# A two-layer decoder trunk on one core: picks in groups of two, a mixer row in every second group, the rotation table beside attention rows, and routings moved between light rows

## The reference, cut to what matters

```
for l in range(2):                                   # DEPTH; x is 256 tokens x 1024
    h = rms_norm(x, norm1_g[l]); proj = h @ w_in[l]  # q, k, v, forget logits, pool, ssm
    att  = forgetting_attention(q, k, v, f_logit + f_bias)      # 8 heads x 64
    pool = multiscale_pool(u_pool)                   # trailing windows 2, 4, 8, 16
    ssm  = s5_mixer(u_ssm)                           # diagonal complex scan, gelu, GLU
    x = x + concat(norm(att), norm(pool), norm(ssm)) @ w_out[l]
    h = rms_norm(x, norm2_g[l])                      # PEER: 128*128 experts, 8 heads, top 16
    q = h @ peer_wq[l]; scores = q . peer_keys[l]    # two halves of 128 keys per head
    e, g = product-key top 16 of each head, softmax  # 8 x 16 = 128 picks per token
    x = x + sum over picks of g * gelu(h . peer_u[l][e]) * peer_v[l][e]
```

## Time and profile before

| engine | busy us | share of the span | instructions |
|---|---|---|---|
| PE (matmul) | 1049.1 | 68% | 6790 |
| PEld (weight load) | 532.8 | 34% | 6790 |
| DVE (VectorE) | 1083.2 | 70% | 2485 |
| ACT (ScalarE) | 575.1 | 37% | 1768 |
| POOL (GpSimd) | 619.7 | 40% | 571 |

### The profile page before, as it was taken

How to read it: one execution, slowest core, us unless ns; L and a number is a source line. 1 busy time by engine, 2 the same in 40 slices (tenths; PEclk the granted TensorE clock), 3 DMA queues, 4 the chain that set the end, 5 groups by cost and what they waited for, 6 DMA issues and landing times. The chain is left out here.

```text
span 1546.1 us, 19439 instructions
## 1 busy us (share of the span) xinstructions
PE 1049.1 (68%) x6790; PEld 532.8 (34%) x6790; DVE 1083.2 (70%) x2485; ACT 575.1 (37%) x1768; POOL 619.7 (40%) x571
## 2 busy tenths in 40 slices
PE   8898656785854668776775667788588465565555
PEld 6685312333531334332552334333255111111111
DVE  8777998646999685654789767564579965444444
ACT  5544433623444433441544431354234432221222
POOL 0034345442753533443343433444243354455441
PEclk9999877887986988787897788889698777667767
DMA  9289999999999999999999999999999999999997
GB/s 381 89 326 421 420 421 420 421 421 405 422 421 368 411 422 421 421 421 421 409 421 421 421 421 421 421 422 420 422 386 421 421 421 422 421 421 422 421 421 304
DMA packets 86642, 623.55 MB, mean 403 GB/s; under 512 B 10000, under 2 KB 10128, under 8 KB 11792
## 3 DMA queue, kind: packets, MB, share of 16 engines
q0 software_dynamic: 73728, 536.90, 83.7%
q1 hardware_dynamic: 12816, 85.41, 13.4%
HBM read 621.23 MB, written 1.05 MB: 402 GB/s over the span
## 5 line engine op out<-in xcount | busy, mean ns | idle before, releaser
L583 POOL DMA_INDIRECT slots<-experts,idx x512 | 593.2, 1159 | 886.5 <-PE psum L1830 709.9
L1427 DVE CUSTOM_DVE_ANT_0 slots<-slots,h 128x1024 f32<-128x1024 f32 x512 | 615.9, 1225 | 390.8 <-DMA slots<-experts,idx 387.6
L1830 PE MATMUL psum<-slots,diag 64*64 64x512 f32 x4088 | 599.3, 737 | 312.4 <-ACT diag L947 312.3
L1830 PEld LDWEIGHTS psum<-slots,diag 64*64 64x64 f32 x4088 | 175.8, 165 | 684.2 <-ACT diag L947 368.9
L931 ACT ACTIVATE ge<-ge 128x4 f32<-128x4 f32 x130 | 26.7, 205 | 437.3 <-DVE ge L1427 436.3
L1752 PE MATMUL psum<-hT,ring 128*128 128x128 f32 x992 | 131.3, 297 | 20.7 <-DMA ring<-weights 16.0
L931 ACT ACT_TABLE_LOAD x55 | 70.6, 1283 | 194.7 <-DVE ge L1427 194.3
L947 ACT ACTIVATE diag<-cst,ge 128x64 f32<-128x64 f32 x511 | 136.5, 336 | 6.7 <-PE psum L1830 2.5
L1752 PEld LDWEIGHTS psum<-hT,ring 128*128 128x128 f32 x992 | 127.7, 212 | 23.5 <-issue 17.7
L938 ACT ACTIVATE ge<-ge,gate 128x1 f32<-128x1 f32 x512 | 109.1, 283 | 4.2
L1525 PE MATMUL psum<-ring,hT 128*128 128x256 f32 x192 | 52.2, 433 | 17.5 <-DVE work L981 17.5
(11 more groups left out here) (292 smaller groups left out, 1075.4 us busy)
## 6 DMA issues: line engine op xcount, KB each, us to landing
ring<-weights SPq DMA_DIRECT2D x32, 1152.0 KB, 10.0
ring<-weights SPq DMA_DIRECT2D x26, 1024.0 KB, 9.2
slots<-weights SPq DMA_DIRECT2D x11, 1024.0 KB, 20.0
slots<-experts,idx POOLq DMA_INDIRECT x512, 20.8
ring<-weights SPq DMA_DIRECT2D x2, 1056.0 KB
sml<-small SPq DMA_DIRECT2D x2, 652.0 KB, 9.1
slots<-weights SPq DMA_DIRECT2D x1, 1056.0 KB, 9.0
xs<-x SPq DMA_DIRECT2D x2, 512.0 KB, 13.2
```

The source lines that it names most:

```text
L583: pool.indirect_dma_start(out=slot[:, place(E), :], out_offset=None, in_=src, in_offset=bass.IndirectOffsetOnAxis(ap=idx[:, n % 2, e:e + 1 ...
L1427: ins = dve.tensor_tensor_reduce(u, u, h2[:, n % 2, :], 1.0, 0.0, ALU.mult, ALU.add, d[:, i:i + 1])
L1830: ins = pe.matmul(acc[HALF * half:HALF * half + HALF, i, :], diag[rows, d % DIAGS, :], slot[rows, place(E), D + half * 512:D + half * 512 ...
```

## The change

- GRP goes from 4 to 2, so there are 64 groups in a step. A row stands only in every second group: after two picks, then two picks without a row, and so on. The weighing, the adds and the semaphores go by groups of two.
- `rows_of(n)` replaces the even spread. Route0 to route5 of the next step run in two runs of three with an empty row between. Route6 and route7 move into the next step, between normA, normT and the u row (rows 2 and 4 of it), so that no group has two rows.
- tab5, tab6 and tab7 move from beside route3 to route5 to beside att0 to att2 of step 1. Part 5 waits for `carry_ready` and `y_psum` of tile 1. The wait for the table moves from ScalarE's normA of step 2 to its sq of step 1.
- The start-up MIX0: the first q chunk is loaded ahead of the constants; mul1, mul2 and mul3 (ScalarE) move behind cum and cm; the reduction of qkn goes ahead of the first scan pieces, of which the second (`scan_im`) and scan1 go behind qkn; in the part for tile 1, route1 and soft1 go behind u, p, qkv0 and qkv1.
- The parameters of layer 1 are loaded after the first routing of step 1 (`routed` 9, before 16).

```diff
-GRP = 4
+GRP = 2
@@ MIX (its last row, ("route0",), goes) and MIX0
-        "power4", "qkv0", "f", "prep", "fx", "ln", "mul0", "mul1", "mul2", "mul3", "rotate0", "rotate1", "cum", "cm",
-        "qkv1", "rotate2", "bu", "qkv2", "scan0", "qkv3", "qkn0", "scan1", "qkn1", "qkv4", "pool", "qkT", "pre0", "pre1",
-        "mixp", "sq1", "scan2", "scan3", "scan4", "scan5", "scan6", "logits0", "scan7", "big0", "logits1", "scan8",
+        "power4", "qkv0", "f", "prep", "fx", "ln", "mul0", "rotate0", "rotate1", "cum", "cm", "mul1", "mul2",
+        "qkv1", "rotate2", "bu", "qkv2", "qkv3", "qkn0", "scan0", "qkn1", "scan_im", "qkv4", "pool", "qkT", "pre0", "pre1",
+        "mixp", "mul3", "sq1", "scan1", "scan2", "scan3", "scan4", "scan5", "scan6", "logits0", "scan7", "big0", "logits1",
...
-        ("xT", 1), ("hTe", 1), "rp1", ("u", 1), "soft0", ("uT", 1), "route1", "soft1", ("p", 1), ("up", 1), ("f", 1),
-        ("fx", 1), ("ln", 1), ("cum", 1), ("cm", 1), ("qkv0", 1), ("qkv1", 1), ("qkv2", 1), ("qkv3", 1), ("qkv4", 1),
+        "route0", ("xT", 1), ("hTe", 1), "rp1", ("u", 1), "soft0", ("uT", 1), ("p", 1), ("up", 1), ("qkv0", 1),
+        ("f", 1), ("fx", 1), ("ln", 1), ("qkv1", 1), "route1", "soft1", ("cum", 1), ("cm", 1), ("qkv2", 1), ("qkv3", 1),
...
@@ MIX1
-        ("att0", "max0", "nrm0"), ("att1", "max1", "nrm1", "mixp"), ("att2", "max2", "nrm2"),
+        ("att0", "max0", "nrm0", "tab5"), ("att1", "max1", "nrm1", "mixp", "tab6"), ("att2", "max2", "nrm2", "tab7"),
         ("att3", "max3", "nrm3"), ("att4", "attg", "sq"), ("merge", "out0"), ("out1", "x1a"),
-        ("out2", "x1p"), ("out3", "x1"), ("h2T", "rp"), ("route0",), ("route1",),
-        ("route2",), ("route3", "tab5"), ("route4", "tab6"), ("route5", "tab7"), ("route6",), ("route7",))
-ROUTES = tuple((f"route{h}",) for h in range(1, PH))
+        ("out2", "x1p"), ("out3", "x1"), ("h2T", "rp"))
+ROUTES = tuple((f"route{h}",) for h in range(PH))
+EMPTY = (0, ())
+def rows_of(n):
+    if n == 0:
+        rows = [(1, r) for r in ((), ("qkn",), ("qkT", "v"))] + [(0, r) for r in ROUTES[2:]] + [(1, r) for r in MIX1]
+    elif n < STEPS - 1:
+        m = n + 1
+        rows = [EMPTY, (m, MIX[0]), (n, ROUTES[6]), (m, MIX[1]), (n, ROUTES[7])] + [(m, r) for r in MIX[2:]]
+    else:
+        return [EMPTY, (n, ROUTES[6]), EMPTY, (n, ROUTES[7])]
+    return rows + [(n + 1, r) for r in ROUTES[0:3]] + [EMPTY] + [(n + 1, r) for r in ROUTES[3:6]]
@@ def script(): (the two lone groups at the end of each step go; one is left at the very end)
-            while at < len(rows) * (quad + 1) // QUADS:
-                step, row = rows[at]
-                order += [("mix", s, 2 if s[:3] == "tab" else step) for s in row]
-                at += 1
+            at, rest = divmod(quad * GRP, 4)
+            step, row = rows[at] if rest == 0 and at < len(rows) else EMPTY
+            order += [("mix", s, 2 if s[:3] == "tab" else step) for s in row]
@@ SyncE
             chunk(CH_POOL)
+            chunk(CH_Q)
             sp.dma_start(cst[:, P:], consts[:, P:]).then_inc(S["cst_in"], 16)
-            for i in range(6):
+            for i in range(1, 6):
...
-                    sp.wait_ge(S["routed"], 2 * PH)
+                    sp.wait_ge(S["routed"], PH + 1)
@@ GpSimd, tab
-                    pool.wait_ge(S["states_ready"], TILES)
+                    pool.wait_ge(S["carry_ready"], TILES)
+                    pool.wait_ge(S["y_psum"], TILES)
@@ ScalarE: normA loses this wait, sq gains it
-                if n == TILES:
-                    act.wait_ge(S["rot_ready"], 2)
+                    if n == 1:
+                        act.wait_ge(S["rot_ready"], 2)
@@ VectorE: a piece of its own for the imaginary half
+            def scan_im(n):
+                link(tt(w3[1], w3[1], w3[3], ALU.subtract))
```

More of the change, by code:

```diff
@@ L116, in script @@
     for n in range(STEPS):
[L117 to L123, removed]
+        rows = rows_of(n)
         for quad in range(QUADS):
@@ L127, in script @@
                 order.append(("mix", "drain", n - 1))
-            done = at
-            while at < len(rows) * (quad + 1) // QUADS:
-                step, row = rows[at]
-                order += [("mix", s, 2 if s[:3] == "tab" else step) for s in row]
-                at += 1
-            order.append(("close", n, quad))
[L134 to L139, removed]
+            at, rest = divmod(quad * GRP, 4)
+            step, row = rows[at] if rest == 0 and at < len(rows) else EMPTY
+            order += [("mix", s, 2 if s[:3] == "tab" else step) for s in row]
+            order.append(("close", n, quad))
+            order += [("mix", "soft" + s[5:], step) for s in row if s[:5] == "route"]
+    return order + [("open", n, QUADS), ("close", n, QUADS), ("mix", "drain", STEPS - 1)]
 ORDER = script()
@@ L191, in experts_of @@
     start, end = PICKS * n + GRP * quad, PICKS * n + GRP * quad + GRP
[L192 to L195, removed]
+    last = PICKS * STEPS - 1
+    return range(start, min(end, last)) if start <= last else range(last, last + 1)
 BY_VECTOR = {PICKS * STEPS - 1}
@@ L203, in by_tensor @@
     return sum(1 for e in range(E) if e not in BY_VECTOR)
-G_LAST = QUADS * STEPS + 1
+G_LAST = QUADS * STEPS
 SECTION = (slice(0, 512), slice(512, 768), slice(768, 1024))
@@ L1116, in scan @@
                     link(tt(w3[0], w3[0], spare, ALU.add))
-                    link(tt(w3[1], w3[1], w3[3], ALU.subtract))
+                if part == 9:
+                    scan_im(n)
                 todo = [(r, b) for r in range(2) for b in range(SB)]
@@ L1428, in dots @@
                 told(ins, "dots_ready")
-            run(dict(inverse=inverse, fold=fold, attg=attg, x1p=x1p, x1a=x1a, h2=h2_, power=power, rotate=rotate_, normA=normA, normT=normT, uT=u_out, cum=cum,
+            run(dict(scan_im=scan_im, inverse=inverse, fold=fold, attg=attg, x1p=x1p, x1a=x1a, h2=h2_, power=power, rotate=rotate_, normA=normA, normT=normT, uT=u_out, cum=cum,
                      warm=blank, h2T=h2T, turnback=turnback, bu=bu, scan=scan, backA=back, backB=back_im, y=y_, glu=glu, qkn=qkn, qkT=qkT,
```

## The result

The changed kernel takes 1557.46 us (median of 5, 1554.81 to 1559.64), the kernel before in the same comparison 1549.18 us (1547.66 to 1553.06): a ratio of 1.0059, 95% interval 1.0044 to 1.0074. It is 8 to 9 us slower. I had forecast 1545.7 us, and my range ended at 1551.5: it is wrong, on the other side. The profiled execution took 1554.81 us with a span of 1553.0, the lowest of the five; it is 6.9 us longer in span than the one of before.

The account below looks back on a forecast made before the run. The prediction took DMA at 421 GB/s as the bound. 1547.98 - 2.0 (start-up) - 11.4 (holes) + 11.3 (table) = 1545.9 us for the profiled execution, so 1545.7 us for the median; range 1535.5 to 1551.5.

Parts of the forecast that it names:

- What bounds the kernel: Whole kernel: DMA at 421 GB/s is the bound, so only time with DMA engines short of work can be won.
- Start-up, -2.0: Before the first gather: qkn's product is ready 2.0 us earlier and everything up to that gather follows, -2.0 us.
- The holes, -11.4: Four mid-run stretches of low DMA traffic, at 340, 465, 745 and 1115 us, would be filled: -11.4 us.
- Groups of two, 0.6 us of wait before a routing's maximum, off the path: Routing rows: VectorE waits 0.6 us for ScalarE's copy of the scores; costs nothing where DMA is the bound.
- The table, +11.3: Table beside attention: part 5 takes 19 us on GpSimd, delays gather 62 and empties the DMA queue; +11.3 us in all.
- part 7: Last table part, beside att2: ends some 22 us after gather 62's issue with 20 us of gathers in front, costing 0.6.
- The rivals: Four cases: table stall 0.50, table nearly hidden 0.27, slower 0.13, slots not freed as said 0.10.
- rival 3: Waits before step 0's routing rows add lag to part 5: stall 17 or more, 1551.5 to 1556 us, chance 0.13.
- the stall: Near 263 us: DMA runs dry while part 5 holds back gather 62; 7 to 15 us, summed at 10.7.

Follow-up runs that it names:

- Experiment 8: The kernel before with only the new order of the first tile's work and first loads: 1545.9 us, ratio 0.9991.
- experiment 1: The changed kernel with the three table parts back beside route3 to route5 of step 1, with their old waits: 1545.18 us, ratio 0.9994.
- experiment 7: The kernel of experiment 1 with GRP = 4 instead of 2: 1546.39 us, ratio 0.9997.
- experiment 3: The changed kernel with GRP = 4 instead of 2: 1556.12 us, ratio 1.0055.
- experiment 2: The kernel before with only the three table parts moved beside att0 to att2, with their new waits: 1557.41 us, ratio 1.0064.
- experiment 12: The kernel of experiment 1 with 14 extra small matmuls (each became two) behind the adds of picks 412 to 507: three executions 1754 to 1756 us, one 1545.95.
- 12-pick pause: The kernel of experiment 1 with the gather of pick 470 waiting for the adds of 12 more picks: 1554.5 us, ratio 1.0058.
- experiment 4: The changed kernel with route6 and route7 of the last step back at the end of the step before: 1559.9 us, ratio 1.0084.

## Why the prediction was wrong, point by point

*What bounds the kernel*: DMA, right. "Only time in which the DMA engines are short of work can be won" is the step that failed, by the way it was measured. I took the mean of sixteen engines; the time is that of the last one.

*Start-up, -2.0*: right in the profile (first gather at 84.16, 2.1 earlier). Experiment 8 gave 1.4 in the time, with an interval that reaches no change.

*The holes, -11.4*: the mechanism was right, since all four were filled, and the term was mis-sized: the four holes were worth 1.6 us, by the sum's row for the kernel before, and nothing clear of noise by the times of experiments 1, 7 and 8. The rest had lain inside the lead. This one term is the error. I had bounded it "between -9 and -11.4", and no bound asked whether a hole costs what it shows; the same trace had the answer in its last microseconds, where the share falls step by step to 0.06 instead of all at once.

*Groups of two, 0.6 us of wait before a routing's maximum, off the path*: seen. VectorE's first maxima idled 28.6 us in all after, 2.7 before, so 0.84 us more in each of 31 routings, put down to ScalarE's copies; experiments 1 and 7 show that it costs nothing:

```profile
L1317 DVE MAX8 ts<-work 128x8 f32<-128x128 f32 x64 | 15.7, 285 | 28.6 <-ACT work L915 14.1
```

I had not foreseen the head of the last step, where groups of two leave one group of 2.5 us between a step's last add and its drain, so that VectorE waits 3.94 us there (in groups of four, experiment 3, it doesn't wait); it too is inside the lead:

```profile
1236.24 2.81 DVE L981 TENSOR_TENSOR xs<-xs,psum 64x512 f32<-64x512 f32 x4 [3.94 <-PE psum L1834]
```

*The table, +11.3*: right. Length 19.2 us for 19, end at 269.0 (in its own frame, with the start 2.1 earlier, I had 269.5), cost 10.5 us in the profile of the changed kernel, 13.1 in its second, 10 to 11 by the times of experiment 2. Within that, part 7 was under-sized (the gap at 290 to 300 us shows 2.4 us, I said 0.6), and a lead of 3 us by the sums, which I did not know of, took as much off again: that the total fits so well is in part luck. On the ports the trace agrees with the rule of the Trainium skill that I cited, "SBUF — State Buffer", "Who interferes with whom", in the form in which the table's many small operations let the dots pass and are stretched by them: 19.2 us where I had estimated 8.3 without them, and two dots held by it for 3.99 and 7.18.

*The rivals*: the median lies just above rival 3's 1551.5 to 1556, and the mechanism is not that of rival 3: VectorE was not later than I had summed. None of my cases had the holes worthless and the stall whole: 1547.98 - 2.0 + 11.3 = 1557.3. That this meets the median of 1557.46 is in part chance: the kernel before took 1.2 us more in that comparison than the number I started from, and the start gave less.

*Still open*: where the lead comes from. Between 245 and 1050 us it grows by some 7 us, so up to there the last engine has nearly one per cent more to do, or is slower by that. Behind 1240 us, where no weight chunk is moved any more, it still grows, but more slowly, by about 0.5 us in 100. So the weight chunks can't be the whole source. The instruction queue, 53 packets of 16 KB, is one candidate, if such a packet goes to one engine (argued, not shown; experiment 12 could not decide it). The Trainium skill, "DMA: Bandwidth & Descriptors", section "Latency and other measured facts", states that engines 7 and 15 are usually slower than the others in traces, and its guess at the cause ties this to transfers whose descriptors GpSimd writes; that is another. No run here shows which engine is the last.

## What to carry to other kernels

Before you sum holes in the mean DMA traffic, look at the last microseconds of it: if the share falls to that of one engine and stays there, the others have a lead, and a hole that is shallower than the lead of its time is free (6.7 us at 1419 here). A short tail proves less: the kernel before has only 2 us of it, since its holes had spent the lead. Time came back here only from the start and from what a hole showed beyond the lead. And what shares GpSimd's queue with gathers must leave them their rate (here one pick per 2.49 us), not merely a gap now and then.

## What I had not expected of the hardware

- The last of the sixteen DMA engines falls behind their middle by some 7 us between 245 and 1050 us, and a pause makes them level again (8.5 us before the 12-pick pause, 1.5 behind it): after that pause the traffic ended in 2 us, without it in 11.
- One engine alone moves its sixteenth of a pick in 2.47 us, which is the pace of all sixteen together; the others' silence doesn't speed it up.
- 28 small matmuls (64x32) a pick, with their weight loads, took TensorE over the pick's 2.49 us at the granted clock of 0.50, and the clock stayed at 0.50 from 1320 to 1700 us with the engine busy all the time. Three executions took over 1754 us (mean granted clock 0.758 to 0.767); in the fourth, with a mean of 0.877, the time was 1545.95 us.
- The profiled execution of the changed kernel was its fastest of five and showed 13.5 us in the table's hole; its second profile showed 16.5, and experiment 4, which is the same kernel up to there, 17.5. One profile of a stall is good to 3 or 4 us here.
